# Late modulation rows one job ahead, gate casts one pair ahead, block sums on VectorE, and the second plain pair's low parts ahead of the norm's sums of squares

## What is computed

```python
h = rmsnorm(x, norm_ffn_g[l])
g = dwconv(jnp.einsum("bsd,df->bsf", h, w_gate[l]), conv_ffn_w[l])
v = jnp.einsum("bsd,df->bsf", h, w_up[l])
x = x + jnp.einsum("bsf,fd->bsd", jax.nn.silu(g) * v, w_down[l])
...
shift, scale, gate = jnp.split(c_act @ ada_w[l] + ada_b[l], 3, axis=-1)
h = modulate(rmsnorm_2(x, norm_g[l]), shift, scale)
```

## Time and profile before

| | |
|---|---|
| median of 3 runs | 2089.79 us (2087.77 to 2091.86) |
| the profiled execution | 2087.84 us |
| its span (first to last instruction) | 2086.1 us |
| mean granted TensorE clock | 0.986 of full speed |
| busy: PE, DVE, POOL, ACT | 96%, 65%, 46%, 33% |

### The profile page before, as it was taken

The page is one execution under the profiler, slowest core; times in us unless marked ns, Lnnn a source line. Parts: engine busy times, 40 slices in busy tenths (PEclk is TensorE's granted clock), DMA queues, the critical chain, the costliest instruction groups (busy, mean ns, idle before and its releaser), DMA issues.

```text
span 2086.1 us, 23855 instructions
## 1 busy us (share of the span) xinstructions
PE 2008.4 (96%) x9084; PEld 1643.3 (79%) x9084; DVE 1364.1 (65%) x1842; ACT 693.2 (33%) x1161; POOL 950.8 (46%) x577
## 2 busy tenths in 40 slices
PE   9999999899999998888899999999999999999998
PEld 7888887677777776766778888888888878777887
DVE  7999678878878874655576545345356372397657
ACT  6323345332332332111045212113122163498212
POOL 4778737556556555333057322222123165265623
PEclk9999999999999999999999999999999999999999
DMA  4231122344433444433211211111111102000102
GB/s 163 68 107 51 41 72 80 111 131 135 134 136 122 131 152 171 144 129 121 93 50 41 71 41 51 51 51 40 50 51 60 31 31 76 11 21 31 61 21 81
DMA packets 54806, 167.55 MB, mean 80 GB/s; under 512 B 6944, under 2 KB 12208, under 8 KB 54704
## 3 DMA queue, kind: packets, MB, share of 16 engines
q1 hardware_dynamic: 42128, 127.94, 18.2%
q10 hardware_dynamic: 12576, 38.23, 5.5%
HBM read 148.30 MB, written 21.00 MB: 81 GB/s over the span
## 4 chain that ended last, share of the span: by engine, by line
PE 69%; POOL 13%; issue 9%; DVE 4%; ACT 3%; DMA 2%; SPq 0%; POOLq 0%; DVEq 0%; ACTq 0%
PE psum L937 20%; PE psum L938 20%; PE psum L939 20%; POOL temp L719 2%; POOL spare_gate_lo L813 2%; POOL w_lo L813 1%; POOL second_sum L828 1%; POOL w_lo L835 1%; DMA temp<-in_ada 1%; POOL spare_raw L824 1%; POOL spare_raw L822 1%; POOL w_raw L824 1%; POOL w_raw L822 1%; ACT probs L1942 1%; PE psum L1343 1%
## 5 line engine op out<-in xcount | busy, mean ns | idle before, releaser
L684 POOL TENSOR_TENSOR w_lo<-w_raw,w_hi 128x1024 fp32r<-128x1024 f32 x131 | 332.4, 2551 | 635.0 <-ACT w_hi L1443 629.5
L937 PE MATMUL psum<-norm_hi,w_hi 128*128 128x512 f32 (+1 forms) x1200 | 469.5, 391 | 26.4 <-DVE stream L2415 26.4
L938 PE MATMUL psum<-norm_lo,w_hi 128*128 128x512 f32 (+1 forms) x1200 | 466.9, 389 | 0.0
L939 PE MATMUL psum<-norm_hi,w_lo 128*128 128x512 f32 (+1 forms) x1200 | 466.5, 389 | 0.0
L937 PEld LDWEIGHTS psum<-norm_hi,w_hi 128*128 128x128 f32 x1200 | 227.6, 190 | 75.3 <-DVE stream L2415 28.5
L939 PEld LDWEIGHTS psum<-norm_hi,w_lo 128*128 128x128 f32 x1200 | 227.4, 190 | 46.6
L938 PEld LDWEIGHTS psum<-norm_lo,w_hi 128*128 128x128 f32 x1200 | 227.7, 190 | 45.9 <-issue 0.2
L2078 DVE SCALAR_TENSOR_TENSOR stream<-psum,mods,stream 128x512 f32<-128x512 f32 x160 | 119.7, 750 | 172.0 <-PE psum L939 172.0
L1443 ACT CAST w_hi<-w_raw 128x1024 fp32r<-128x1024 f32 x114 | 116.1, 1048 | 334.6 <-PE psum L939 207.3
L2415 DVE TENSOR_TENSOR stream<-psum,stream 128x512 f32<-128x512 f32 x176 | 119.2, 687 | 70.7 <-PE psum L939 70.3
L2166 DVE SCALAR_TENSOR_TENSOR psum<-glu,vec,psum 128x1024 f32<-128x1024 f32 x116 | 149.6, 1290 | 4.1
(11 more groups left out here) (312 smaller groups left out, 4209.9 us busy)
## 6 DMA issues: line engine op xcount, KB each, us to landing
w_raw<-in_slabs SPq DMA_DIRECT2D x155, 512.0 KB, 3.3
ada_raw<-in_ada ACTq DMA_DIRECT2D x18, 1024.0 KB, 4.9
temp<-in_ada ACTq DMA_DIRECT2D x28, 512.0 KB, 4.2
spare_raw<-in_slabs SPq DMA_DIRECT2D x20, 512.0 KB, 3.9
ffn_y_scratch<-ffn_y SPq DMA_DIRECT2D x18, 512.0 KB, 5.1
sum_raw<-ffn_y_scratch SPq DMA_DIRECT2D x5, 1024.0 KB, 6.4
stream<-in_x SPq DMA_DIRECT2D x8, 512.0 KB, 9.0
stream_scratch<-stream SPq DMA_DIRECT2D x8, 512.0 KB, 2.8
```

The costliest lines, as they stand in the source:

```text
L684: nc.gpsimd.tensor_tensor(WL[place][:, :], RAW[at % 2][:, :], WH[place][:, :].bitcast(f32), ALU.subtract).then_inc(slab_ready, 1)
L937: nc.tensor.matmul(dst, wh, xh, start=n == 0, stop=False)
L938: nc.tensor.matmul(dst, wh, xl, start=False, stop=False)
L939: last = nc.tensor.matmul(dst, wl, xh, start=False, stop=n == len(terms) - 1)
```

## The change

Four edits:

1. ScalarE issues the late rows' loads of job n-2 behind the casts of job n, from n = 3 on, where it issued those of job n-3 from n = 4 on. VectorE sums the rows behind tiles 3, 8 and 13, not 2, 7 and 12 (the fourth of job 9 stays behind tile 15).
2. `gate_cast(1)` comes ahead of the loop over the pairs, and in the loop `gate_cast(n + 2)` comes behind `s1_cast(n + 1)`, where `gate_cast(n + 1)` came ahead of `s2_cast(n + 1)`.
3. POOL takes the low parts of slabs 30 and 31 ahead of `sums(FFN)`.
4. The two differences `t1_raw`, the first `last_low` and the low parts of the third block sum go from POOL to VectorE; VectorE's block sums are split, the first two ahead of `gate_times_up(0)` and the others behind it, and the convolution of tile 1 comes ahead of the low parts `extra_low(2, ...)`. The semaphore `t3_lo` is gone, and TensorE waits for `extra_lo` at 8 instead.

```diff
@@ POOL
-            lows(25, FFN_SLAB + 2)
+            lows(25, FFN_SLAB + 4)
             sums(FFN)
-            lows(FFN_SLAB + 2, FFN_SLAB + 4)
             piece_low(FFN, 9)
             piece_low(FFN, 11)
             piece_low(FFN, 13)
-
-            for pair in range(2):
-                gp.wait_ge(norm_done, 8 + 2 * pair + 2)
-                gp.wait_ge(lo_done, 8)
-                nc.gpsimd.tensor_tensor(t1_raw(pair), block_of(0, 1, pair), block_of(0, 0, pair), ALU.subtract
-                                        ).then_inc(t1_made, 1)
...
-            gp.wait_ge(s34_hi, 1)
-            nc.gpsimd.tensor_tensor(WL[3][:, :], seven_raw(0)[0][:, :], WH[3][:, :].bitcast(f32), ALU.subtract
-                                    ).then_inc(s34_lo, 1)
-            for pair in range(2):
-                gp.wait_ge(extra_hi, 7 + pair)
-                nc.gpsimd.tensor_tensor(extra(EXL, 1, pair), extra(EX_RAW, 1, pair),
-                                        extra(EXH, 1, pair).bitcast(f32), ALU.subtract).then_inc(t3_lo, 1)
@@ ScalarE
             corner_cast(3, 0)
             corner_cast(3, 1)
+            gate_cast(1)
...
                 if last:
                     row_cast(0)
                 else:
-                    gate_cast(n + 1)
                     s2_cast(n + 1)
                 if last:
                     row_cast(1)
                 else:
                     s1_cast(n + 1)
+                    if n + 2 < SEVENS:
+                        gate_cast(n + 2)
...
-                if n > 3:
-                    for i in late_rows(n - 3):
+                if n > 2:
+                    for i in late_rows(n - 2):
                         if i + 2 < LATE_ROWS:
                             load_late(i + 2)
-            for job in (len(JOBS) - 3, len(JOBS) - 2):
-                for i in late_rows(job):
-                    if i + 2 < LATE_ROWS:
-                        load_late(i + 2)
+            for i in late_rows(len(JOBS) - 2):
+                if i + 2 < LATE_ROWS:
+                    load_late(i + 2)
@@ VectorE
+            first_sums()
             dve.wait_ge(act_read, 44)
             gate_conv(0)
-            extra_sums()
+            dve.wait_ge(pool_low, pool_lows(FFN, 15))
+            dve.wait_ge(tiles, FFN_TILE)
+            extra_sums(2)
             gate_times_up(0)
+            extra_sums(4)
+            extra_sums(3)
             extra_low(0, 0, 1)
             extra_low(0, 1, 2)
             y_low(0)
             t1_low(0, 3)
             t1_low(1, 4)
             sum_low(0)
+            dve.wait_ge(act_read, 48)
+            gate_conv(1)
             extra_low(2, 0, 5)
             extra_low(2, 1, 6)
-            dve.wait_ge(act_read, 48)
-            gate_conv(1)
...
-                if n:
-                    last_low(n)
+                last_low(n)
...
                 add(first, bank[1], mixed_gate, [(tiles, t + 2), (part_kept, n + 1)])
+                if n == 0:
+                    extra_low(1, 0, 7)
+                    extra_low(1, 1, 8)
...
-                if j in (2, 7, 12, 15) and (2, 7, 12, 15).index(j) < len(rows):
-                    late_row(rows[(2, 7, 12, 15).index(j)])
+                if j in (3, 8, 13, 15) and (3, 8, 13, 15).index(j) < len(rows):
+                    late_row(rows[(3, 8, 13, 15).index(j)])
```

More of the change, by code:

```diff
@@ L298, in build @@
         f_conv, f_silu, f_mul, f_hi, f_lo = (sem(n) for n in ("f_conv", "f_silu", "f_mul", "f_hi", "f_lo"))
-        t1_made = sem("t1_made")
         gate_in = [sem(f"gate_in{n}") for n in range(2)]
@@ L303, in build @@
             sem(n) for n in ("gate_hi", "gate_lo", "sums_made", "s2_hi", "s2_lo", "s1_hi", "s1_lo", "s34_hi", "s34_lo"))
-        extra_made, extra_hi, extra_lo, t3_lo = (
-            sem(n) for n in ("extra_made", "extra_hi", "extra_lo", "t3_lo"))
+        t1_made, extra_made, extra_hi, extra_lo = (
+            sem(n) for n in ("t1_made", "extra_made", "extra_hi", "extra_lo"))
         part_kept, part_added = sem("part_kept"), sem("part_added")
@@ L1149, in seven_products @@
                 if n == 0:
-                    pe.wait_ge(t3_lo, 2)
+                    pe.wait_ge(extra_lo, 8)
                 product(bank[2], WH[3], WL[3], 0, *extra_part(1))
@@ L2277, in _, with first_sums, extra_sums @@
             apply(FFN, 16 - STAT_AT[FFN])
-            def extra_sums():
+            def first_sums():
                 dve.wait_ge(norm_done, 16)
                 dve.wait_ge(lo_done, dve_lows(FFN, 15))
-                dve.wait_ge(pool_low, pool_lows(FFN, 15))
-                dve.wait_ge(tiles, FFN_TILE)
-                for n, left, right in ((0, lambda p: block_of(1, 1, p), t1_raw),
-                                       (2, lambda p: block_of(1, 0, p), lambda p: extra(EX_RAW, 0, p)),
-                                       (1, lambda p: block_of(1, 1, p), lambda p: block_of(0, 1, p))):
-                    for pair in range(2):
-                        if n == 0:
-                            dve.wait_ge(t1_made, pair + 1)
-                        if n == 2:
-                            dve.wait_ge(extra_made, made(2, pair))
-                        nc.vector.tensor_tensor(extra(EX_RAW, n, pair), left(pair), right(pair), ALU.subtract
-                                                ).then_inc(extra_made, 1)
+                for pair in range(2):
+                    nc.vector.tensor_tensor(t1_raw(pair), block_of(0, 1, pair), block_of(0, 0, pair), ALU.subtract
+                                            ).then_inc(t1_made, 1)
+            def extra_sums(n):
+                for pair in range(2):
+                    if n == 2:
+                        dve.wait_ge(t1_made, pair + 1)
+                        left, right = block_of(1, 1, pair), t1_raw(pair)
+                    elif n == 4:
+                        dve.wait_ge(extra_made, made(2, pair))
+                        left, right = block_of(1, 0, pair), extra(EX_RAW, 0, pair)
+                    else:
+                        left, right = block_of(1, 1, pair), block_of(0, 1, pair)
+                    nc.vector.tensor_tensor(extra(EX_RAW, n - 2, pair), left, right, ALU.subtract).then_inc(extra_made, 1)
             def extra_low(n, pair, cast):
@@ L2355, in last_low @@
                 dve.wait_ge(s34_hi, n + 1)
-                dve.wait_ge(s34_lo, n)
                 nc.vector.tensor_tensor(WL[3][:, :], seven_raw(n)[0][:, :], WH[3][:, :].bitcast(f32), ALU.subtract
                                         ).then_inc(s34_lo, 1)
+            first_sums()
             dve.wait_ge(act_read, 44)
             gate_conv(0)
-            extra_sums()
+            dve.wait_ge(pool_low, pool_lows(FFN, 15))
+            dve.wait_ge(tiles, FFN_TILE)
+            extra_sums(2)
             gate_times_up(0)
+            extra_sums(4)
+            extra_sums(3)
             extra_low(0, 0, 1)
```

## The result

The changed kernel takes **2015.69 us** (median of 4 runs, 2015.02 to 2016.62) against 2089.56 (4 runs beside it, 2087.77 to 2091.86). The ratio is 0.9646, with a 95% interval of 0.9629 to 0.9663: 73.9 us are gone. The profiled execution has a span of 2013.4 us and a mean granted clock of 0.995 (2086.1 and 0.986 before), so the two traces differ by 72.7.

A forecast was written before the change was run, and what follows sets the result against it. TensorE bound it, busy 2008.4 of 2086.1 us, its idle time mostly waits on VectorE's adds. Gains of 48.0 + 16.2 + 0.8 + 4.5 = 69.5 us off 2087.84 gave 2018.3, stated as 2020; range 2010 to 2036.

The forecast's parts named there:

- Late rows: Down jobs: loads one job ahead end five of six TensorE waits, job 1's shortened; 48.0 us gained, bounds 36.9 to 50.
- Gate casts: Pairs: gate casts one pair ahead remove the whole 0.90 us lost per pair; 16.2 us gained, bounds 0 and 16.2.
- Rival A: The pairs keep their 0.90 us, VectorE's queue having little room; 2036 us, chance 0.12.
- Low parts ahead of the sums: Ahead of the pairs: first spread 1.1 us late, second spread's 1.89 us wait gone; 0.8 us gained, bounds -2.0 and +1.9.
- Block sums: From five instructions moved to VectorE: TensorE gains 1.3 us at 379.22 and 393.61, loses 408.00's wait; 4.5 together, bounds -1, +9.
- rival C: More gained than forecast: job 1's wait without slow clock, the wait at 393.61 gone too; 2013 us, chance 0.05.
- B: Down jobs: row waits partly return, ScalarE held by a row's sum and late with a cast; 2038 us, chance 0.07.
- D: Pairs: gate cast ahead of the tap waits for its load; slower, 2146 us at 15 us a load, chance 0.02.
- E: Down jobs: no effect, since loads still leave at the job's end; chance 0.02 for no change that can be told.

## Why the prediction was right

The forecast of 2020 us was 4.3 too high, 0.2%, and on the right side. Term by term:

- **Late rows, 48.0 forecast, 47.4 between the traces, 49.4 by undoing it.** Job 1 kept its wait, as worked out: 2.97 us idle for 3.3, and 1.9 of slow clock where I had added 1.0. That 1.9 is not fixed: in the run with the low parts behind the sums a wait of 2.85 us there had no slow matmuls behind it. The other five waits went. That the rows may stand at either set of tiles once the loads are early was shown by the run with only the rows back.
- **Gate casts, 16.2 forecast, 16.2 between the traces.** The chain came out at 22.3 us after the pair's first matmul (548.89 - 526.60), where I had 22.7, and the room is 2.2 us for 1.8. VectorE's low part began 0.2 us later in the pair than worked out, but took 1.43 us and not the 2.20 that I had kept from the trace before. Rival A, the pairs keep their 0.90 us, fell; its reason did not. It said that the slack goes if POOL's steps fall on VectorE's work elsewhere, and the runs with one and three more low parts show just that. In the changed kernel the low part at 541.49 starts 1.0 us ahead of POOL's gate low part and keeps its 1.43 us; an instruction more on VectorE comes behind the start of it.
- **Low parts ahead of the sums, 0.8 forecast, 1.5 measured** (between the traces, and again by undoing it). The price was right (the first spread is 1.1 us later), the gain was 2.6 and not 1.9: from the first spread to the second it is 13.64 us (334.22 - 320.58) with the edit and 16.21 (335.67 - 319.46) without.
- **Block sums, 4.5 forecast, 7.9 between the traces.** This term was mis-sized, and it mixed two edits. The wait at 408.00 went, by the early gate cast: 3.8 us in pair 1 where I had 3.2. At 379.22 and 393.61 I had 1.3 us gained, and the waits did shrink by that (0.68, and 3.19 to 2.54). But pair 0 gained 4.1 us. The other 2.7 are slow matmuls that follow the wait of 3.19 us in the trace before and not the one of 2.54 after; I had counted them only for the case in which the wait goes, in the upper bound and in rival C, and it stayed. That they stayed away is luck: in two of nine traces with this same wait they came, and cost 1.6 us. Nor did I see that the early gate cast costs pair 0 some 1.3 us and the block sums give it 5.4.
- **Rivals B, D, E.** No row of jobs 3 to 7 waits for its load, so B and E fall. D, a gate cast late for its load, did not come up: no tap waits behind a load, and the cast ran at 541.35, as the prediction's 14.7 us into the pair had it. How slow a load would have to be was not tried.

The sum was 69.5 where the traces differ by 72.7: 3.4 and 0.7 too little in the last two terms, 0.6 too much in the first, and 0.3 lost elsewhere. The medians differ by 1.2 more than the traces do, which is within the spread of the runs.

The exclusion of VectorE and POOL, which the prediction took from the earlier trace rows for one instruction, carries more of this kernel than I gave it. Before, two early rows took 2.83 and 2.30 us (from 550.34 on) beside POOL's gate low part and weight sums; now each takes 1.22 (from 532.85 on). The rule of the Trainium skill, page "SBUF — State Buffer", section "Who interferes with whom", says that the ports which VectorE and GpSimd share are an exclusive lock, and that the one that issues first has them for its whole instruction while the other is blocked. The collisions shown here agree: 3.31 and 1.23 us for one instruction, and 5.67 or 4.64 for POOL's two by who came first.

## What to carry to other kernels

Room in a chain is not room for an instruction: look first at what GpSimd runs at that time, since a VectorE instruction with two SBUF inputs that begins second costs its own time plus what is left of GpSimd's (3.31 us for 1.2 here). When a transfer is late, look at what stands ahead of it in the queue that issues it; issuing the rows' loads one job's casts earlier gave 47 to 49 us here, and moving three of them ahead of one more blocked cast gave 4.9. And count the slow matmuls behind a wait with the wait, as a range and not as a number: here the same wait had them in one execution and not in another.

## What the runs showed of the hardware

TensorE's granted clock did not follow from the length of the wait alone. Slow matmuls (0.63 us, 0.43 apart, at a granted clock of 0.50) came behind waits of 2.50, 2.97, 3.19, 4.17 and 5.29 us, and none behind 2.54 us in the changed kernel or 3.15 us in the one before. Nor did the place decide it. At the third add of pair 0 nine traces have a wait of 2.52 to 2.54 us: slow matmuls follow in two of them (the low parts behind the sums, and the three more low parts) and not in the other seven. Behind job 1's wait of 2.85 us they follow in the run with the gate casts back and not in the one with the low parts behind the sums. So the same wait costs 1.6 us more in one execution than in another. What decides it these runs don't show.

And of two orders of VectorE and GpSimd that lie a few tenths of a microsecond apart, one makes a row 1.25 us long and the other 3.30.
